# Another order of loads and of tensor work in a loop over pairs of experts, with the down weights in fewer, larger loads

## The reference

```
logits = xt @ w_router + b_router
top_p, top_e = top_k(softmax(logits), 2)        # top_p normalised to sum 1
for each expert e, for the rows xb sent to it:
    y = (silu(xb @ w_gate[e]) * (xb @ w_up[e])) @ w_down[e]
out[row] = sum over its two experts of top_p * y
x = x + g_f * out;  y = rmsnorm(x, norm_out)
```

## Time and profile before

| | |
|---|---|
| median of 3 runs | 1340.59 us (1339.93 to 1341.5) |
| profiled execution | 1340.71 us, span 1339.0 us |
| TensorE (PE) busy | 1238.2 us, 92% of the span |
| VectorE, ScalarE, GpSimd busy | 215.6, 123.2 and 23.5 us |
| mean DMA rate | 345 GB/s over the span; 462.23 MB moved |
| chain that ended last | PE 74%, DMA 19%, issue 3%, VectorE 2% |

### The profile page before, as it was taken

How to read it: one execution, slowest core, us unless ns; L and a number is a source line. 1 busy time by engine, 2 the same in 40 slices (tenths; PEclk the granted TensorE clock), 3 DMA queues, 4 the chain that set the end, 5 groups by cost and what they waited for, 6 DMA issues and landing times.

```text
span 1339.0 us, 27624 instructions
## 1 busy us (share of the span) xinstructions
PE 1238.2 (92%) x12330; PEld 711.6 (53%) x12331; DVE 215.6 (16%) x595; ACT 123.2 (9%) x245; POOL 23.5 (2%) x113
## 2 busy tenths in 40 slices
PE   6899999999998699876799999998999988999885
PEld 3777788877885543234453334664333555333553
DVE  0298200000005501010110202001010002010002
ACT  2201410000002310000001000000000001000002
POOL 1000100000001000000000000000000000000000
PEclk9899999999999999889889999998999998999999
DMA  9999675556436399999998899998999999999993
GB/s 332 410 403 392 212 277 202 205 178 228 163 115 251 115 385 417 419 421 424 418 402 340 340 420 422 421 402 348 405 419 419 423 418 418 419 418 419 421 421 146
DMA packets 87886, 462.23 MB, mean 345 GB/s; under 512 B 8748, under 2 KB 12120, under 8 KB 52664
## 3 DMA queue, kind: packets, MB, share of 16 engines
q1 hardware_dynamic: 85937, 456.41, 85.5%
q10 hardware_dynamic: 1814, 3.85, 0.8%
HBM read 458.94 MB, written 2.24 MB: 344 GB/s over the span
## 4 chain that ended last, share of the span: by engine, by line
PE 74%; DMA 19%; issue 3%; DVE 2%; ACT 1%; POOL 1%; SPq 0%; DVEq 0%; ACTq 0%; POOLq 0%
PE bank L1624 32%; PE bank L1389 25%; DMA ring<-in_w_exp_down_dram 17%; PE bank L1646 7%; PE bank L1583 3%; PE bank L1358 2%; DMA ring<-in_w_exp_up_dram 2%; PE bank L1673 1%; PE bank L1282 1%; PE bank L1514 0%; DVE xT L949 0%; SPq L530 0%; ACT MIX L882 0%; DVE BIG L421 0%; PE bank L1525 0%
## 5 line engine op out<-in xcount | busy, mean ns | idle before, releaser
L1624 PE MATMUL bank<-ring,HT 128*32 128x512 f32 (+1 forms) x5120 | 490.7, 544 | 14.4 <-DMA ring<-in_w_exp_up_dram 9.9
L1624 PEld LDWEIGHTS bank<-ring,HT 128*32 128x32 f32 x5120 | 165.0, 110 | 336.6 <-issue 304.6
L1389 PE MATMUL bank<-HT,ring 128*128 128x264 f32 x1024 | 232.6, 389 | 2.5 <-POOL HT L621 2.5
L1389 PEld LDWEIGHTS bank<-HT,ring 128*128 128x128 f32 x1024 | 194.4, 191 | 43.3 <-issue 10.5
L1646 PE MATMUL bank<-ring,hid_t 128*32 128x256 f32 x2560 | 148.9, 379 | 5.9 <-DMA ring<-in_w_exp_down_dram 5.8
L1646 PEld LDWEIGHTS bank<-ring,hid_t 128*32 128x32 f32 x2560 | 90.5, 110 | 57.0 <-issue 10.7
L1389 PE MATMUL bank<-BIG,ring 128*128 128x264 f32 x480 | 107.3, 386 | 0.0
L1646 PE MATMUL bank<-ring,COND 128*32 128x256 f32 x1344 | 81.3, 389 | 23.7 <-DMA ring<-in_w_exp_down_dram 23.7
L1389 PEld LDWEIGHTS bank<-BIG,ring 128*128 128x128 f32 x480 | 91.1, 190 | 15.5
L1221 DVE TENSOR_TENSOR bank<-bank,hid_t 128x512 f32<-128x512 f32 (+1 forms) x22 | 13.9, 630 | 385.0 <-PE bank L1624 385.0
L1646 PEld LDWEIGHTS bank<-ring,COND 128*32 128x32 f32 x1344 | 43.5, 111 | 60.4 <-DMA ring<-in_w_exp_down_dram 33.9
(11 more groups left out here) (225 smaller groups left out, 494.0 us busy)
## 6 DMA issues: line engine op xcount, KB each, us to landing
ring<-in_w_exp_gate_dram SPq DMA_DIRECT2D x64, 1024.0 KB, 17.1
ring<-in_w_exp_up_dram SPq DMA_DIRECT2D x64, 1024.0 KB, 14.2
ring<-in_w_exp_down_dram SPq DMA_DIRECT2D x64, 1024.0 KB, 26.8
ring<-in_w_ada_dram SPq DMA_DIRECT2D x48, 1024.0 KB, 14.0
ring<-in_w_exp_gate_dram SPq DMA_DIRECT2D x64, 768.0 KB, 17.1
ring<-in_w_exp_up_dram SPq DMA_DIRECT2D x64, 768.0 KB, 15.9
ring<-in_w_exp_down_dram SPq DMA_DIRECT2D x32, 1536.0 KB, 28.6
ring<-in_w_in_dram SPq DMA_DIRECT2D x10, 1024.0 KB, 25.7
```

Of the source, the lines that this page charges most:

```text
L1389: ins = t_.matmul(banks_of[label][:, 0:NT], w[:, k, f * P:(f + 1) * P], src(k0 + k), start=(k0 + k == 0), stop=(k0 + k == k_tiles - 1))
L1624: ins = t_.matmul(bank[GATE_BANKS[role][g]][i * GRP:(i + 1) * GRP, 0:cols], xg[:, k, c0:c0 + GRP], w[:, :, i * cols // QUAD:(i + 1) * cols ...
```

## The change

It has four parts.

1. **Loads ahead of the flags.** The first expert's gate and up loads now stand first in `LOADS` (16 of 1 MiB), and SP waits for the flags ahead of load 16 where it was load 8. So all 14 MiB of the ring are filled before the flags are known.
2. **Order of phases.** For each half: large gate, large up, small gate, small up. So a stretch of one expert is 16 loads long where it was 8. Banks are dealt out anew.
3. **Rotated loop.** `gather` and `take_batch` of a pair are done in the pair before it, between the second and third load of the first large down; for the first pair they are done ahead of the flags. They always take all 224 columns, where they took as many as the variant has. Of `place`, the large expert's part for the first 512 features stands in the middle of the last small down.
4. **Down loads.** Half 0 comes in 4 loads of four rows a partition (2 MiB, 16 KB in one piece, pieces 64 KB apart) where it was 8 loads of two rows (8 KB pieces 16 KB apart). Half 1 keeps 4 loads of three rows (12 KB), now 48 KB apart where they lay side by side. A partition now holds adjacent features, so the gate matmul reads 512 adjacent weights and VectorE's transpose takes another stride.

```diff
-DOWN_PARTS = (2, 2, 2, 2, 2, 2, 2, 2, 3, 3, 3, 3)
+DOWN_PARTS = (4, 4, 4, 4, 3, 3, 3, 3)
 DOWN_UNITS = len(DOWN_PARTS)
 HALVES = {"large": (0, 1), "small": (1, 0)}
-PHASES = tuple((role, kind, HALVES[role][f])
-               for kind, f in (("gate", 0), ("up", 0), ("gate", 1), ("up", 1), ("down", 0), ("down", 1)) for role in ROLES)
-DOWN_LOADS = (range(0, 8), range(8, DOWN_UNITS))
+PHASES = tuple((role, kind, HALVES[role][f]) for f in range(2) for role in ROLES for kind in ("gate", "up")) + tuple(
+    (role, "down", HALVES[role][f]) for f in range(2) for role in ROLES)
+DOWN_LOADS = (range(0, 4), range(4, DOWN_UNITS))
...
-GATE_BANKS = {"large": (0, 1, 2, 3, 4), "small": (5, 6)}
-OUT_BANKS = {"large": (0, 1, 2), "small": (7,)}
+GATE_BANKS = {"large": (0, 1, 4, 5, 6), "small": (2, 3)}
+OUT_BANKS = {"large": (4, 5, 6), "small": (7,)}
...
-            down_0 = w_exp_down[0][:, 0:split1, :].rearrange("e (j p i) d -> e j p (i d)", j=QUAD, p=P)
-            down_1 = w_exp_down[0][:, split1:DFE, :].rearrange("e (j p i) d -> e j p (i d)", j=QUAD, p=P)
+            down_0 = w_exp_down[0][:, 0:split1, :].rearrange("e (p i) d -> e p (i d)", p=P)
+            down_1 = w_exp_down[0][:, split1:DFE, :].rearrange("e (p i) d -> e p (i d)", p=P)
...
-                    if first and n == DT:
+                    if first and n == 2 * DT:
...
-                        src = down_0[e, i // 2, :, (i % 2) * size:(i % 2 + 1) * size] if i < 8 else down_1[e, i - 8]
+                        src = down_0[e, :, i * size:(i + 1) * size] if i < 4 else down_1[e, :, (i - 4) * size:(i - 3) * size]
...
+                    if first and n < RING:
+                        sp.wait_ge(ring_used, UNITS0 - (RING - 1 - n))
+                    elif (role, kind, i) != ("small", "gate0", 0):
...
+            def take_batch(p):
+
                 for b in GATHER_BANKS:
                     act.wait_ge(on("gathered"), p * 4 + (b + 1))
-                    src = bank[b][:, 0:2 * BOTH].rearrange("p (t n) -> p t n", t=2)[:, :, here]
-                    a.activation(xg[:, 2 * b:2 * b + 2, here], src, ACT.Copy).then_inc(on("xg_ready"), 1)
+                    src = bank[b][:, 0:2 * BOTH].rearrange("p (t n) -> p t n", t=2)
+                    a.activation(xg[:, 2 * b:2 * b + 2, :], src, ACT.Copy).then_inc(on("xg_ready"), 1)
...
+                take_batch(p + 1)
...
+            take_batch(0)
...
-                return prod.rearrange("p (j b i) -> p j i b", j=QUAD, b=GRP)
+                return prod.rearrange("p (b j) -> p j b", b=GRP)
...
+            def gather(p):
...
+                            ins = t_.matmul(bank[b][:, i * BOTH:(i + 1) * BOTH], h_rows[:, t, d * P:(d + 1) * P], pick[t][:],
+                                            start=(i == 0 and t == 0), stop=(t == 2), skip_group_check=True)
                     ins.then_inc(on("gathered"), 1)
+
+            gather(0)
+            pe.wait_ge(on("flags_ready"), 1)
+            passes = pe.value_load(flag[0:1, 2 * NE:2 * NE + 1], min_val=1, max_val=2)
...
+                        pe.wait_ge(on("x_updated"), p * DT + (GATE_BANKS[role][g] + 1))
+                        if GATE_BANKS[role][g] in GATHER_BANKS:
+                            pe.wait_ge(on("xg_ready"), p * 4 + (GATE_BANKS[role][g] + 1))
...
-                                                xg[:, k, c0:c0 + GRP], w[:, :, i * cols // QUAD:(i + 1) * cols // QUAD],
-                                                start=(k == 0), stop=(k == DT - 1))
+                                                xg[:, k, c0:c0 + GRP], w[:, i, :], start=(k == 0), stop=(k == DT - 1))
...
+                        if u in between:
+                            between[u]()
...
+                def place_part(role, h, frees=False):
+                    groups = count[role]
+                    for g in range(groups):
+                        at = g + (L if role == "small" else 0)
+                        for i in range(QUAD):
+                            ins = t_.matmul(bank[PLACE_BANKS[h][i]][:, 0:NT],
+                                            out_rows[i * GRP:(i + 1) * GRP, at, h * P:(h + 1) * P],
+                                            place[at][i * GRP:(i + 1) * GRP, :], start=(role == "large" and g == 0),
+                                            stop=(role == "small" and g == groups - 1))
+                            if frees and g == 0 and i == 0:
+                                ins.then_inc(ring_used, 1)
+                            if role == "small" and g == groups - 1:
+                                ins.then_inc(on("scattered"), 1)
+
+                def next_gather():
+                    pe.wait_ge(on("small_hidT"), p * 2 * S + 2 * S)
+                    gather(p + 1)
+
+                def place_large_first_half():
+                    pe.wait_ge(on("place_ready"), p * GMAX + GMAX)
+                    pe.wait_ge(on("large_rows_ready"), p * 2 + 2)
+                    pe.wait_ge(on("xg_ready"), (p + 1) * 4 + 4)
+                    place_part("large", 0)
+
                 for s in range(2):
                     for role in ROLES:
-                        down(role, s)
-
-                pe.wait_ge(on("place_ready"), p * GMAX + GMAX)
-                pe.wait_ge(on("large_rows_ready"), p * 2 + 2)
-                for h in range(2):
-                    for role in ROLES:
-                        for g in range(count[role]):
-                            if (h, role, g) == (0, "small", 0):
-                                pe.wait_ge(on("small_rows_ready"), p + 1)
-                            at = g + (L if role == "small" else 0)
-                            for i in range(QUAD):
-                                ins = t_.matmul(bank[PLACE_BANKS[h][i]][:, 0:NT],
-                                                out_rows[i * GRP:(i + 1) * GRP, at, h * P:(h + 1) * P],
-                                                place[at][i * GRP:(i + 1) * GRP, :], start=(role == "large" and g == 0),
-                                                stop=(role == "small" and g == count["small"] - 1))
-                                if (h, role, g, i) == (0, "large", 0, 0):
-                                    ins.then_inc(ring_used, 1)
-                                if role == "small" and g == count["small"] - 1:
-                                    ins.then_inc(on("scattered"), 1)
+                        for kind in ("gate", "up"):
+                            expand(role, kind, s)
+                down("large", 0, {DOWN_LOADS[0][2]: next_gather})
+                down("small", 0)
+                down("large", 1)
+                down("small", 1, {DOWN_LOADS[0][2]: place_large_first_half})
+
+                pe.wait_ge(on("small_rows_ready"), p + 1)
+                place_part("small", 0)
+                place_part("large", 1, frees=True)
+                place_part("small", 1)
...
```

26 lines of the change are left out of this document (3 added, 23 removed).

## The result

The changed kernel is slower. Its median over five runs is 1348.35 us (1343.22 to 1348.97), that of the kernel before, over five runs beside it, 1340.59 us (1339.93 to 1341.5): the ratio on record is 1.0046, 95% interval 1.0032 to 1.0061, so 4 to 8 us more (the two medians by themselves are 7.8 us apart). Two later sets of runs gave 1.0039 (1.0025 to 1.0053) and 1.0036 (1.0022 to 1.0049). I had forecast 1335.2, within 1329 to 1343.5.

A forecast was written before the change was run, and what follows sets the result against it. The prediction took the pair loop to be bound by the weight stream. Its terms, -4.3 - 5.8 + 2.6 + 1.0 - 1.8 + 1.5 + 1.3 = -5.5 us, took 1340.7 to 1335.2 us, range 1329 to 1343.5.

The forecast's parts named there:

- second rival: Last pair's downs: TensorE becomes the bound; 1344 us if the gather falls to half clock; chance 0.12.
- 70.7 us TensorE: Last pair's downs: TensorE's down work, gather and place total 70.7 us, against 70.0 us for the stream.
- +1.3: End of the kernel: the 2 MiB last load lengthens the tail, place shortens it by 0.4; net +1.3 us.
- the sign of a right forecast: Last downs: TensorE would be seen waiting for loads.
- -5.8: Second pair and gaps between pairs: shorter gaps shrink the stream's pauses, -5.8 us (0 to -12).
- 1.5 us in the ring and 1.7 at the end: 2 MiB down loads: needing 2 MiB free at once costs 1.5 us, the larger last load 1.7 us.
- First expand 472.5: Ahead of the loop: with the gather before the flags, the first expand begins near 472.5 us.
- -4.3: Start: the next load goes out at 475.1 us instead of 479.4, -4.3 us (-5.7 to +0.7).
- this edit alone is worth nothing: Loads ahead of the flags: both kernels have 14 MiB in the ring when TensorE starts, so no gain.
- +2.6 and +1.0: Phase order: pauses in the first and third pairs' long stretches, +2.6 us; small expert's Silu waits, +1.0 us (0 to 4).
- third rival: Down loads: the spaced 16 KB pieces run slowly, 4.2 us more instead of 1.8 less, 1341 us; chance 0.06.
- -1.8: Down loads: 16 KB pieces instead of 8 KB save fixed cost, 1.1% of 160 us, -1.8 us.

The follow-up runs named there:

- e8: Changed kernel with the next pair's gather moved from the downs into the small expert's last expands, bank by bank; 1341.67 us, ratio 1.0001 to the kernel before.
- e9: The changed kernel unedited, run again on another set's chip; 1347.68 us, ratio 1.0036 to the kernel before.
- e6: Changed kernel with half 0's down loads as 8 of two rows (1 MiB) for 4 of four rows (2 MiB); 1339.83 us, ratio 0.999.
- e10: Changed kernel with the gather in the small expert's last expands and two-row (1 MiB) down loads in half 0; 1341.35 us, ratio 0.9997.
- e1: The changed kernel unedited, run once more; 1346.1 us, ratio 1.0039 to the kernel before.
- e2: Changed kernel whose gathers inside the loop do one of three row tiles, 8 matmuls for 24; 1345.07 us, ratio 1.0026.
- e4: Changed kernel with the gather put back at the start of its own pair; 1355.91 us, ratio 1.0111.
- e5: Changed kernel with large and small expand phases in turn again, flags read after 8 loads; 1342.58 us, ratio 1.0006.
- e15: Changed kernel with first halves' phases as changed, second halves' large and small in turn, 2 MiB down loads kept; 1344.19 us, ratio 1.0023.
- e13: Changed kernel with two-row (1 MiB) down loads in half 0 and the flags read after 8 loads; 1344.88 us, ratio 1.0027.
- e7: Changed kernel with phases in turn, flags read after 8 loads, and two-row (1 MiB) down loads in half 0; 1339.82 us, ratio 0.999.
- e11: Changed kernel with gather in the small expert's last expands, two-row (1 MiB) down loads and phases in turn; 1341.08 us, ratio 0.9993.
- e12: Changed kernel with gather in the small expert's last expands and phases in turn, 2 MiB down loads kept; 1340.99 us, ratio 0.999.

## Why the prediction was wrong

**The end.** The gather in the last downs was the prediction's second rival, and it is the case that came. The step that failed is its balance of "70.7 us TensorE" against "the stream needs 70.0", from which the sum took only "+1.3" for the tail. Both sizes were near: TensorE's last down ends at 1314.35 + 7.09 = 1321.4, 71.8 us after the downs begin, where I had 70.7. What was wrong is that the two don't start together. The stream's 70.0 us hold the first load, and TensorE starts when that has landed. From there the stream has 26 MiB left, 27.3 MB at 425 GB/s, 64 us. In the trace the weights are in at 1314 us (last columns: clock, DMA share, GB/s):

```profile
1313.00:1314.00 1.00, 1.00 (x24) 0.86 (x20) 0.00 (x0) 0.00 (x0) 0.00 (x0) 1.00 0.08 33
1314.00:1315.00 1.00, 1.00 (x24) 0.47 (x20) 0.00 (x0) 0.00 (x0) 0.00 (x0) 1.00 0.00 0
```

So TensorE ends 7 us behind the stream. Not all of that is loss, since the last 2 MiB load is 3.66 us of TensorE wherever the gather stands. e8 gives the measure: its last down, behind the last load, ends at 1319.5, 1.9 us before the changed kernel's 1321.4 and 5.4 before e9's 1324.9. The rest of the 9.28 us of gather falls into time in which TensorE would have waited.

And the first load was made twice as large. The timeline of TensorE in the changed kernel, idle time and its releaser in brackets:

```profile
1249.65 10.57 PE L1648 MATMUL bank<-ring,hid_t 128*32 128x256 f32 x192 [3.07 <-DMA ring<-in_w_exp_down_dram]
```

and the same place in e6 (the view ends at 1256 us, so its row is cut short there):

```profile
1246.43 9.92 PE L1648 MATMUL bank<-ring,hid_t 128*32 128x256 f32 x180 [0.65 <-DMA ring<-in_w_exp_down_dram]
```

2.4 us more of waiting, for 1 MiB of stream. Without the gather such a wait is free, since the downs wait for later loads anyway; e8 against e10 (1.0001 and 0.9997) shows it free as far as these runs can tell. With the gather there each us of it goes to the end. It can cost twice: TensorE idles 3.07 us, and in e9 it came back at half clock. Timeline and then windows of e9, last columns granted clock, DMA share, GB/s:

```profile
1250.26 13.46 PE L1648 MATMUL bank<-ring,hid_t 128*32 128x256 f32 x192 [3.07 <-DMA ring<-in_w_exp_down_dram]
```

```profile
1246.00:1250.00 4.00, 1.19 (x12) 0.13 (x4) 2.72 (x4) 0.00 (x0) 0.00 (x0) 0.92 1.02 434
1250.00:1254.00 4.00, 3.74 (x36) 2.03 (x40) 0.00 (x0) 0.00 (x0) 0.00 (x0) 0.50 0.99 422
```

The same 192 records take 13.46 us instead of 10.57: +2.9, which is the 76.34 less 73.45 of the table. The level there is 1.2 GHz. After the same wait of 3.06 to 3.08 us the clock fell in e9, e1, e2 and e4, for 1.7 to 2.9 us of cost, and not in the changed kernel's first profile, e5 or e15.

In e8 the downs begin 3.5 us later than in the changed kernel, behind the copies to `xg` (a wait of 1.20 us for ScalarE), and end sooner:

```profile
1253.17 13.16 PE L1654 MATMUL bank<-ring,hid_t 128*32 128x256 f32 x240 [1.20 <-ACT HT L838]
...
1315.87 3.66 PE L1654 MATMUL bank<-ring,COND 128*32 128x256 f32 x64 [0.92 <-DMA ring<-in_w_exp_down_dram]
```

TensorE waits for weights again up to the last load, which is what I had named as the sign of a right forecast. The changed kernel has no such row behind its first down.

**The second pair.** The step that failed is "-5.8" for the gap between the pairs, where a gather leaves and the pauses shrink. The count of the lead took the stream as what the time follows, though the prediction itself had the pair at 217 us of TensorE against 210. In such a pair the pauses are a sign, not a cost (they did shrink, by 3 us over the stretches above). Windows of the changed kernel over the pair from first expand to last down:

```profile
668.30:743.00 74.70, 74.03 (x708) 27.63 (x708) 10.29 (x22) 3.48 (x6) 0.00 (x0) 1.00 0.93 361
743.00:797.00 54.00, 54.00 (x672) 21.90 (x676) 1.15 (x2) 2.45 (x5) 0.00 (x0) 1.00 1.01 415
797.00:817.00 20.00, 16.88 (x168) 4.98 (x156) 6.72 (x12) 0.60 (x1) 0.00 (x0) 1.00 1.00 397
817.00:903.60 86.60, 86.40 (x1432) 57.57 (x1432) 0.69 (x1) 3.07 (x7) 0.00 (x0) 0.98 0.95 390
```

TensorE is busy 231.3 of 235.3 us. A gather moved from behind this pair to inside it is 9.28 us of TensorE for 9.80: nothing is gained, whatever the stream does in the gap. And there are two kinds of new waits, for the 2 MiB load and for ScalarE. TensorE's waits from 668 to 900 us, by what released them (the first stands ahead of the first expand, in the gap, where TensorE idled for 4.74 us before):

```profile
PE bank L1624 <- DVE tmp L952: 2.5, 1, 2.5
PE bank L1648 <- DMA ring<-in_w_exp_down_dram: 2.4, 1, 2.4
PE bank L1624 <- ACT COND L846: 1.5, 2, 0.8
```

Row by row against the earlier trace rows: expand takes 146.4 us (668.27 to 814.7) for 144.46, of which 1.5 is the small expert's wait for its Silu; then 2.4 for the first 2 MiB load; then downs, gather and place 90.3 us (817.11 to 907.4) for 72.52 + 5.59 + 9.80 = 87.9. In sum +6.8 of the +6.90. The last 2.4 hold a stretch at half clock behind the wait (the 0.98 in the last window; the first 320 records of down take 19.16 us for 17.47 in e6) and the hand-over of place.

The 2 MiB loads, which I had priced at 1.5 us in the ring and 1.7 at the end, cost 5.2 us of loop in the changed kernel against e6 and 7.1 in e9. These are the waits where TensorE bounds, 2.42 us for e6's 1.05 in the second pair and 3.07 for 0.65 in the last, and what half clock adds behind one of them (1.7 us in the changed kernel, 2.9 in e9).

**The start.** "First expand 472.5" was right in the profile (471.91) and near in the two others (475.28, 473.51). Against the 475.74 of before that is -3.8, -0.5 and -2.2. The -4.3 was counted at the next load, which was to go out at 475.1. In the changed kernel it went out at 477.23 for 479.39, -2.2 us, since the first expands ran at half clock:

```profile
477.23 2.90 SPq L532 DMA_DIRECT2D ring<-in_w_exp_up_dram  x2
```

```profile
473.00:476.00 3.00, 3.00 (x17) 0.82 (x13) 0.00 (x0) 1.18 (x1) 0.00 (x0) 0.50 0.81 332
```

And the reasoning had a hole: "this edit alone is worth nothing" of the loads ahead. The first row of expand and the stretch of DMA ahead of it, in e6:

```profile
473.86 10.51 PE L1624 MATMUL bank<-ring,HT 128*32 128x512 f32 x96 [3.00 <-issue]
```

```profile
460.00:475.00 15.00, 12.00 (x67) 10.94 (x70) 0.00 (x0) 2.33 (x5) 0.00 (x0) 0.93 0.17 51
```

and in e13, which differs in how many loads go ahead of the flags:

```profile
478.82 5.87 PE L1624 MATMUL bank<-ring,HT 128*32 128x512 f32 x28 [6.53 <-issue]
```

```profile
460.00:475.00 15.00, 12.29 (x62) 11.83 (x61) 0.91 (x5) 2.18 (x4) 0.00 (x0) 0.89 0.99 401
```

TensorE goes from the gather through the reading of the flags and its branch with the DMA engines nearly idle in one, at 401 GB/s in the other, and takes 3.00 and 6.53 us. In the sixteen profiles with the first gather ahead of the flags (all but before and e4) this idle time is 2.98 to 3.46 us in ten of the eleven with 14 loads ahead (the eleventh is e2), and 5.64 to 6.53 in the five with 8. So e5, e7, e11 and e12 pay back at the start part of what their order gains in the loop. Of e13's 5 us, 3.5 are this idle time; the gather ahead of it ends 1.4 us later. That the traffic of the DMA engines is what lengthens the branch is an inference: the edit also moves SP's own reading of the flags. The Trainium skill says in "Runtime: NRT & Kernel Launch", section "Instruction fetch mechanics", that a branch to a page which is not at hand forces a DMA fetch of it; a fetch that has to share its engines with weights would look like this, but no row here shows the fetch itself. Why e2 took 10.30 us with its ring full stays open.

**Pauses of the long stretches.** +2.6 and +1.0: the Silu waits are 1.5 us in the second pair and reach TensorE's time in full. The order of phases, with the flags read as early as each order allows, is worth 0.3% with 2 MiB loads (e5 against the changed kernel's 1.0036 to 1.0046, 4 us) and nothing with 1 MiB loads (e7 against e6). By itself it is worth more: with the flags read after 8 loads in both, e7 against e13 gives 5 us with 1 MiB loads, where the prediction had 3.6 for its two terms. What the long order gains by its 14 loads ahead it loses in the loop.

**Down loads.** The third rival falls. Loads whose 16 KB pieces lie 64 KB apart run at 424 to 426 GB/s, those before at 421 to 424. The Trainium skill's rule on row pitch ("DMA: Bandwidth & Descriptors", "Latency and other measured facts"), by which I had estimated up to 5 us, is not seen at 64 KB. The -1.8 shows in no time: in e8 and e10, where the stream bounds the end again, 2 MiB and 1 MiB loads give 1.0001 and 0.9997.

Put together: the -4.3 came, by the first expand, as -2.2 in the mean of three profiles, the -5.8 as nothing, and the loop as +5.3, +8.3 and +7.2 (changed, e1, e9). That makes +1.5, +7.8 and +5.0, where the medians say +5 to +8. Of the second rival I had the mechanism, and the sign that would show it ("TensorE without waits from the third pair's downs on") holds for the downs of the third and of the last pair. I gave it 0.12 because I took 70.7 against 70.0 for a tie.

## What to carry to other kernels

Before work is moved from a gap into a stretch, ask which engine sets that stretch's end, once for every pass of the loop: here it was hidden in the first pair, neutral in the second and third, and in the last it was 9.3 us of new work for a pass that doesn't exist, of which some 2 us reached the end at full clock, and 5 with a stretch at half clock. A larger load is waited for whole, and that is free only where its reader has time to spare; so test such edits in pairs, since each of three edits undone alone took away nearly all of a loss that they made together, and look for what else an edit moves, as the order of phases moved the reading of the flags. The whole change but for its 2 MiB loads (e6) is as fast as the kernel before, and none of fourteen variants was faster beyond what these runs can tell.
